# A two-layer transformer kernel on one NeuronCore: the last tile of each layer norm in two token halves

## The reference, cut to what matters

```
mod = silu(c) @ w_ada[l] + b_ada[l]            # six vectors of 1024: sh1, sc1, g1, sh2, sc2, g2
h = x * (1 + sc1) + sh1
y = token_mixer(h, ...)                        # ends in merged @ w_out
x = layer_norm(ALPHA * x + g1 * y, ln1_g, ln1_b)
h = x * (1 + sc2) + sh2
y = conv_ffn(h, ...)                           # ends in u @ w_down, 2816 rows
x = layer_norm(ALPHA * x + g2 * y, ln2_g, ln2_b)

def layer_norm(x, g, b):                       # over the 1024 features of each token
    mu = mean(x); var = mean((x - mu) ** 2)
    return (x - mu) * rsqrt(var + 1e-5) * g + b
```

## Time and profile before

| | |
|---|---|
| median of 3 runs | 2410.18 us (2404.59 to 2410.34) |
| profiled execution | 2407.2 us, its span 2404.8 us |
| TensorE busy | 2337.0 us, 97% of the span |
| VectorE, ScalarE, GpSimd busy | 1265.6 (53%), 992.3 (41%), 995.6 (41%) us |
| mean granted TensorE clock | 0.997 |
| DMA | 259.54 MB, mean 108 GB/s |

### The profile page before, as it was taken

One profiled execution on the slowest core, in us unless ns is written; L12 is line 12 of the kernel. 1 busy time (PEld: TensorE's weight loads), 2 busy tenths in 40 slices (PEclk: granted clock), 3 DMA queues, 4 the chain that ended last, 5 costly groups with the idle time before them and its releaser, 6 DMA issues.

```text
span 2404.8 us, 32261 instructions
## 1 busy us (share of the span) xinstructions
PE 2337.0 (97%) x11392; PEld 1866.7 (78%) x11392; DVE 1265.6 (53%) x2662; ACT 992.3 (41%) x1649; POOL 995.6 (41%) x808
## 2 busy tenths in 40 slices
PE   6999999999999999999999999999999999999988
PEld 4778778878888876887787888887888867778756
DVE  7575675654445356657567434314640163276684
ACT  6444445344343244544534343423142344333463
POOL 3343222454444443423244544444544434454342
PEclk9999999999999999999999999999999999999999
DMA  8532134322226334212442232223232221222210
GB/s 332 214 123 71 61 115 158 123 73 102 93 88 236 106 149 160 97 36 88 144 146 96 88 105 89 88 96 112 88 105 87 102 78 36 87 88 88 88 45 36
DMA packets 51843, 259.54 MB, mean 108 GB/s; under 512 B 6352, under 2 KB 16080, under 8 KB 26128
## 3 DMA queue, kind: packets, MB, share of 16 engines
q1 hardware_dynamic: 50576, 249.63, 29.9%
q0 software_dynamic: 1152, 8.39, 0.8%
HBM read 249.47 MB, written 7.34 MB: 107 GB/s over the span
## 4 chain that ended last, share of the span: by engine, by line
PE 77%; issue 11%; POOL 5%; DVE 4%; ACT 2%; DMA 1%; SPq 0%; POOLq 0%; DVEq 0%; ACTq 0%
PE bank L738 22%; PE bank L740 21%; PE bank L739 21%; POOL w_lo L595 4%; PE bank L986 2%; PE bank L899 1%; PE bank L1225 1%; PE bank L991 1%; PE bank L1028 1%; PE bank L888 1%; PE bank L874 1%; PE bank L929 1%; PE bank L1214 1%; PE bank L1377 1%; DMA ada_early<-w_ada 0%
## 5 line engine op out<-in xcount | busy, mean ns | idle before, releaser
L595 POOL TENSOR_TENSOR w_lo<-w_raw,w_hi 128x512 fp32r<-128x512 f32 (+1 forms) x684 | 873.1, 1308 | 1208.3 <-ACT w_hi L1429 815.6
L738 PE MATMUL bank<-h_hi,w_hi 128*128 128x512 f32 x1616 | 647.0, 400 | 11.5 <-ACT gates_b L1509 5.6
L740 PE MATMUL bank<-h_hi,w_lo 128*128 128x512 f32 x1616 | 631.4, 391 | 0.0
L739 PE MATMUL bank<-h_lo,w_hi 128*128 128x512 f32 x1616 | 629.8, 390 | 0.0
L738 PEld LDWEIGHTS bank<-h_hi,w_hi 128*128 128x128 f32 x1616 | 304.3, 188 | 85.4 <-issue 18.4
L740 PEld LDWEIGHTS bank<-h_hi,w_lo 128*128 128x128 f32 x1616 | 303.7, 188 | 64.9
L739 PEld LDWEIGHTS bank<-h_lo,w_hi 128*128 128x128 f32 x1616 | 304.4, 188 | 58.3 <-issue 0.5
L1429 ACT ACTIVATE w_hi<-w_raw 128x2048 fp32r<-128x2048 f32 (+2 forms) x112 | 197.6, 1764 | 280.5 <-PE bank L740 227.6
L2293 DVE SCALAR_TENSOR_TENSOR cv<-bank,par,cv 128x511 f32<-128x511 f32 (+1 forms) x176 | 131.6, 749 | 213.4 <-ACT cv L1685 200.4
L1434 ACT ACTIVATE w_hi<-w_raw 128x2048 fp32r<-128x2048 f32 x68 | 129.9, 1910 | 125.5 <-PE bank L740 117.0
L1685 ACT ACTIVATE cv<-bank,par 128x512 f32<-128x512 f32 x88 | 68.3, 779 | 233.4 <-PE bank L740 232.1
(11 more groups left out here) (385 smaller groups left out, 3841.1 us busy)
## 6 DMA issues: line engine op xcount, KB each, us to landing
w_raw<-w_stream SPq DMA_DIRECT2D x150, 1024.0 KB, 4.9
w_raw<-w_down SPq DMA_DIRECT2D x32, 704.0 KB, 4.0
ada_mid<-w_ada SPq DMA_DIRECT2D x20, 1024.0 KB, 5.4
ada_last<-w_ada SPq DMA_DIRECT2D x12, 1024.0 KB, 4.9
ada_early<-w_ada POOLq DMA_DIRECT2D x8, 1024.0 KB, 20.8
ada_late<-w_ada SPq DMA_DIRECT2D x8, 1024.0 KB, 6.3
bias_in<-bias_scratch SPq DMA_DIRECT2D x16, 256.0 KB, 3.0
bias_in<-bias_scratch SPq DMA_DIRECT2D x16, 192.0 KB, 2.7
```

The source lines that it names most:

```text
L595: ins = nc.gpsimd.tensor_tensor(w_lo[r][:, part], w_raw[r][:, part], w_hi[r][:, part].bitcast(fp32), ALU.subtract)
L738: nc.tensor.matmul(out, w[0][:, cols], xh, start=first, stop=False)
L739: nc.tensor.matmul(out, w[0][:, cols], xl, start=False, stop=False)
L740: return nc.tensor.matmul(out, w[1][:, cols], xh, start=False, stop=last)
```

## The change

Tile 7 is computed in two halves of 256 tokens, each to its end, in different banks. For each half DVE adds the residual, then adds it to `ln_shift`; ACT squares the half; DVE adds the square to `ln_mean`. `norm_early` is gone: behind the tile one set of sums is made from the complete `ln_shift` and `ln_mean`, by token for the first half and then for the second, then 512 columns for the mean. In the second norm, DVE adds the first slot's part of tile 7 as a whole while the second slot runs in halves.

In the tail, ACT copies the next slot's high part in four pieces of 512 columns, one behind each of the first four high parts of the activation, and POOL subtracts the mean from tiles 2 to 7 rather than 3 to 7.

In the first norm of a layer, the group behind tile 5 makes four sums; the other eight (gate columns 40 to 47) are made in the tail where the last five warming products were, and DVE takes them after the tail. `ada_take` and `affine` move ahead of the residual of tile 6.

```diff
 # GpSimd, norm_sub
-                for f in range(3, KD):
+                for f in range(2, KD):
...
 # TensorE
-            def tile(out, w, at, xh, xl, ks, k0=0, first=True, last=True):
+            def tile(out, w, at, xh, xl, ks, k0=0, first=True, last=True, tok=slice(0, S)):
                 for k in range(ks):
-                    ins = mm3(out, w, slice(at + k * P, at + (k + 1) * P), xh[:, k0 + k, :], xl[:, k0 + k, :],
+                    ins = mm3(out, w, slice(at + k * P, at + (k + 1) * P), xh[:, k0 + k, tok], xl[:, k0 + k, tok],
                               first and k == 0, last and k == ks - 1)
...
-            def norm_early(l, which):
-                k = 2 * l + which
-                pe.wait_ge(zcsum_ready, k + 1)
-                nc.tensor.matmul(banks[5][:, :], mean_w, ln_shift[:, :], start=True, stop=False)
-                by_token(4, ln_shift)
-                pe.wait_ge(sq_used, KD * k + 7)
-                by_token(3, ln_mean).then_inc(early_done, 1)
...
                 elif f == 7:
-                    pe.wait_ge(tile_evac, tdone(l, t + 6))
-                    keep_warm(0, 3)
-                    pe.wait_ge(tile_evac, tdone(l, t + 7))
-                    by_token(2, x[:, 7, :]).then_inc(tok_done, 1)
-                    pe.wait_ge(sq_ready, KD * (k + 1))
-                    by_token(7, ln_sq[1]).then_inc(sq_used, 1)
-                    nc.tensor.matmul(banks[5][:, :], mean_w, x[:, 7, :], start=False, stop=True).then_inc(rest_done, 1)
+                    for c in range(2):
+                        pe.wait_ge(zcsum_ready, 4 * k + 2 + 2 * c)
+                        ins = by_token(2, ln_shift, HALF_BLOCKS[c])
+                        if c:
+                            ins.then_inc(tok_done, 1)
+                            pe.wait_ge(sq_used, KD * (k + 1))
+                        else:
+                            pe.wait_ge(zcsum_ready, 4 * k + 3)
+                        ins = by_token(7, ln_mean, HALF_BLOCKS[c])
+                    ins.then_inc(tok_done, 1)
+                    nc.tensor.matmul(banks[5][:, :], mean_w, ln_shift[:, :], start=True, stop=True).then_inc(rest_done, 1)
                     pe.wait_ge(inv_ready, k + 1)
...
-                    keep_warm(0, 5)
+                    if which:
+                        keep_warm(0, 5)
+                    else:
+                        pe.wait_ge(ada_used, 2 * (12 * l + 12))
+                        ada_products(6, 2, 0, 7).then_inc(ada_sum, 1)
...
                     else:
-                        tile(banks[1][:, :], split(l, SLOT_OUT + 3), D, m_hi, m_lo, 5, last=False)
-                        norm_early(l, 0)
-                        ins = tile(banks[1][:, :], split(l, SLOT_OUT + 3), D + 5 * P, m_hi, m_lo, 3, 5, first=False)
+                        for c in range(2):
+                            if c:
+                                pe.wait_ge(tile_evac, tdone(l, TILE_OUT + 6))
+                            ins = tile(banks[1 - c][:, HALF[c]], split(l, SLOT_OUT + 3), D, m_hi, m_lo, KD, tok=HALF[c])
+                            if c == 0:
+                                ins.then_inc(half_done, 1)
...
-                        ada_group(12 * l + 9, 3, 0, 6)
+                        ada_group(12 * l + 9, 1, 0, 6)
...
+                        if f == 7 and s:
+                            for c in range(2):
+                                if c:
+                                    pe.wait_ge(part_added, 3 * l + 2)
+                                else:
+                                    pe.wait_ge(tile_evac, tdone(l, TILE_DOWN + 6))
+                                tile(banks[c][:, HALF[c]], split(l, SLOT_DOWN + s), 0, u_hi, u_lo, 11, 11, tok=HALF[c]
+                                     ).then_inc(tile_done if c else half_done, 1)
...
 # ScalarE, norm_tail
-                split_hi(l, *split_after)
                 act.wait_ge(gb_ready, k + 1)
+                n = slot_no(l, split_after)
+                act.wait_ge(w_full[n % 2], 16 * (n // 2 + 1))
                 for j in range(KD):
                     act.wait_ge(zn_ready, k * KD + j + 1)
                     A_(h_hi[:, j, :], banks[2 + j % 2][:, :], ACT.Identity, bias=ln_gb[:, 8 + j:9 + j]).then_inc(h_hid, 1)
+                    if j < 4:
+                        part = slice(512 * j, 512 * j + 512)
+                        ins = A_(w_hi[n % 2][:, part], w_raw[n % 2][:, part], ACT.Copy)
+                        if j == 3:
+                            ins.then_inc(w_hi_done, 1)
...
 # VectorE, in place of the residual of tile 7
+            def last_residual(l, which, t):
+                k = 2 * l + which
+                scale = mod[l][:, 23 + 24 * which:24 + 24 * which]
+                if which:
+                    dve.wait_ge(half_done, HALVES * (l + 1) - 1)
+                    V.scalar_tensor_tensor(x[:, 7, :], banks[1][:, :], scale, x[:, 7, :], ALU.mult, ALU.add
+                                           ).then_inc(part_added, 1)
+                    dve.wait_ge(part_added, 3 * l + 2)
+                dve.wait_ge(zcsum_ready, 4 * k + 1)
+                dve.wait_ge(sq_used, KD * k + 7)
+                for c in range(2):
+                    at = HALF[c]
+                    if c:
+                        dve.wait_ge(tile_done, tdone(l, t + 7))
+                    else:
+                        dve.wait_ge(half_done, HALVES * l + (2, HALVES)[which])
+                    V.scalar_tensor_tensor(x[:, 7, at], banks[c if which else 1 - c][:, at], scale, x[:, 7, at], ALU.mult,
+                                           ALU.add).then_inc(tile_evac if c else part_added, 1)
...
+                    V.tensor_tensor(ln_shift[:, at], x[:, 7, at], ln_shift[:, at], ALU.add).then_inc(zcsum_ready, 1)
+                    dve.wait_ge(sq_ready if c else sq_half, KD * (k + 1) if c else k + 1)
+                    V.tensor_tensor(ln_mean[:, at], ln_sq[1][:, at], ln_mean[:, at], ALU.add
+                                    ).then_inc(sq_used if c else zcsum_ready, 1)
...
 # VectorE, norm_tail
-                        if f >= 3:
-                            dve.wait_ge(zs_ready, 5 * k + f - 2)
+                        if f >= 2:
+                            dve.wait_ge(zs_ready, 6 * k + f - 1)
...
-                    if f == 7:
+                    if f == 6:
                         ada_take(l, 2)
                         affine(l, 0)
...
                 norm_tail(l, 0)
+                dve.wait_ge(ada_sum, 4 * l + 4)
+                chain(V.tensor_tensor(mod[l][:, 40:48], banks[7][:, 0:256:32], par[l][:, 40:48], ALU.add))
```

More of the change, by code:

```diff
@@ L49 @@
  TILE_DOWN, TILES) = (0, 8, 16, 24, 28, 32, 40, 44, 52, 60, 68, 76, 120, 128)
-HALVES = 9
+HALVES = 11
 SLOT2_Q, SLOT2_V, SLOT2_GATE, SLOT2_OUTA, SLOT2_K2, SLOT2_V2, SLOT2_Q2, SLOT2_G2, SLOT2_OUTB, SLOTS2 = (
@@ L339, in build @@
         var_ready = sem("var_ready")
-        early_done = sem("early_done")
+        part_added = sem("part_added")
+        sq_half = sem("sq_half")
         tok_done = sem("tok_done")
@@ L441, in build @@
                ("k", 3)]
+        HALF, HALF_BLOCKS = (slice(0, S // 2), slice(S // 2, S)), (range(2), range(2, NB))
         OUT_FIRST = (7, 4)
@@ L774, in keep_warm, with ada_products @@
                     nc.tensor.matmul(banks[bank][:, 0:P], ones, ident, start=True, stop=True)
-            def ada_group(first, halves, late, bank):
-                pe.wait_ge(ada_used, 2 * (first + halves))
-                part = first % 12 - 4 if first % 12 else 0
+            def ada_products(part, halves, late, bank):
                 for j in range(4 * halves):
@@ L782, in ada_group @@
                                            ones[:, 0:32], start=True, stop=True)
-                ins.then_inc(ada_sum, 1)
+                return ins
+            def ada_group(first, halves, late, bank):
+                pe.wait_ge(ada_used, 2 * (first + halves))
+                ada_products(first % 12 - 4 if first % 12 else 0, halves, late, bank).then_inc(ada_sum, 1)
             pe.sem_inc(tile_done, TILE_PRE)
@@ L925, in stat, with by_token @@
                 return nc.tensor.matmul(banks[bank][:, :], w, src, start=(f == first), stop=(f == KD - 1))
-            def by_token(bank, src):
-                for b in range(NB):
+            def by_token(bank, src, blocks):
+                for b in blocks:
                     ins = nc.tensor.matmul(banks[bank][:, b * P:(b + 1) * P], src[:, b * P:(b + 1) * P], mean_w,
@@ L1145, in down @@
                             wait_bank(l, TILE_DOWN + f, 2)
[L1146 to L1149, removed]
+                        if f == 7 and s:
[7 more added lines that the diff above has]
+                        else:
+                            ins = tile(banks[f % 2][:, :], split(l, SLOT_DOWN + s), 0, u_hi, u_lo, 11, 11 * s, s == 0,
+                                       s == 1 or f == 7)
+                            ins.then_inc(tile_done if s else half_done, 1)
                 for f in range(KD):
```

(35 more changed lines are left out.)

18 lines of the change are left out of this document (8 added, 10 removed).

## The result

The changed kernel takes 2389.02 us (median of four runs, 2388.77 to 2390.99) against 2409.82 for the kernel before (2404.59 to 2410.34): ratio 0.992, 95% interval 0.9903 to 0.9938. Timed once more later: 2388.34 against 2405.8, ratio 0.9926 (0.9913 to 0.994), which is 17.5 us. The profiled execution took 2389.18 us (span 2387.0) where the one of before took 2407.2. The forecast was 2392.

What follows compares the result with a forecast made beforehand. Most of the kernel was taken to be a TensorE stream, 77% of the span. First norms 4.45 and second norms 3.83, twice each, take 16.6 us off 2407.2, so 2390.6; forecast 2392, range 2385 to 2397.

Steps and rivals of the forecast that it cites:

- steps 1 and 2: Last tile of each norm: no early sums, gain 2.56 us; two halves, cost 0.31 us (first norms) or 0.43 (second).
- step 3: First norm of each layer: 16 of 24 narrow products behind tile 5 move into the gap, gain 0.5 us.
- the margin at the second half: First norm's last tile: DVE done with the first half at 474.9, TensorE with the second at 475.5, margin 0.6 us.
- steps 4 and 5: Each norm: shorter tail to the variance, gain 0.7 us; weight split in pieces and POOL's extra subtraction, gain 1.0 us.
- Halves do not fall back: Last tile: 256-column products not half the time of whole ones; 2409 at 0.20 us (chance 0.07), 2455 at 0.40 (0.04).
- DVE is held by POOL: Last tile: POOL holds DVE's first-half sums 1.1 us each, giving 2398; chance 0.13 together with nothing from steps 4 and 5.
- The clock did not fall behind a gap: Rival, gap behind the last tile: granted clock falls to 0.50, 1.4 us each at two norms, so 2395; chance 0.08.
- the basis: Time of the kernel before: profiled 2407.2, 3.0 below the median 2410.18; 2390.6 from the profiled one, forecast 2392.

Runs made afterwards that it cites:

- gates_early: The changed kernel with all 24 narrow products behind tile 5 of each first norm again, ten warming products in the gap: 2390.02 us.
- whole_tile: The changed kernel with the last tile of each norm whole again, one set of sums behind it: 2393.68 us.
- best: The changed kernel with 32 narrow products split, tile 4's residual ahead of DVE's centring, gate sum and affine coefficients in DVE's waits behind the last residual: 2383.92 us.
- pool_later: The changed kernel with POOL's low part in second norms held until DVE's two first-half sums are done: 2392.15 us.
- widths: The changed kernel with 96 more fp32r products of eight widths in one gap of layer 0's first norm: spacing 0.228 us at 512 columns, 0.120 at 256.
- copy_whole: The changed kernel with ACT copying the 2048-column weight whole ahead of the high parts: next slot 0.45 us later in norms 1, 2 and 4.

## Why the prediction was right

**Early sums, split (steps 1 and 2): right.** The end of the last tile came 2.76 us sooner behind the narrow products, forecast 2.56 - 0.31 + 0.5 = 2.75. That the two agree to 0.01 is partly luck: the late gate columns gave 0.40 of it and not 0.5, and the early sums cost TensorE 2.36 + 0.32 = 2.68 (gates_early and whole_tile) and not the 2.56 of the pause itself. No run puts the early sums back into the change; the 2.68 is a difference of timelines. The split cost 0.32 us (whole_tile), forecast 0.31, and 0.43 in norm 4, forecast 0.43; the form that no row showed takes 0.120 us, as assumed. The Trainium skill ("TensorE: Matmul & The Clock Gate", "Back-to-back issue gap") would make the split cost 48 x 0.098 - 24 x 0.131 = 1.56 us, an estimate from its figures; the measurement disagrees and decides.

**Late gate columns (step 3): right in kind, a little too large.** 0.39 us instead of 0.5 per first norm; the rest is the 1.23 us wait for DVE that the forecast named, and best shows that it can be had. What the step got wrong is a margin: the gate columns and affine coefficients do not fit ahead of the residual of tile 6. From 469.58 on they take DVE 1.46 us, forecast about 1; the tile's last product ends at 470.37 + 0.39 = 470.76, and DVE starts the residual at 471.04 with no wait, so about 0.25 us late. With another 0.20 between DVE's last sum of squares and the first half's residual, for which the forecast had nothing, the margin at the second half is 0.20 us instead of 0.6. It cost nothing, but little was left.

**Tail and pieces (steps 4 and 5): right.** 2.27 us from residual to variance, forecast 2.3. From the tile's end to the next slot it takes 18.28 us instead of 20.02: 1.74 less, forecast 1.7. The parts add up to 1.67: 0.70 from the tail, 0.45 from the pieces and 0.52 from POOL's sixth subtraction. POOL's low part ends at 493.55, 1.24 us ahead of the next slot, forecast 1.2.

**The rivals.** Halves do not fall back. DVE is held by POOL in the second norms as feared, by 1.07 us a sum, and still has 0.41 us to spare. The forecast had judged the hold against the first norm's margin of 0.6; in norm 2 DVE waits 2.41 us for the second half when the first half's sums are not held (pool_later), which also shows the price where the hold is not covered. The two sums from which the forecast inferred the hold differ in their operands as well, the short one reading a bank; pool_later compares like with like. The clock did not fall behind a gap in any norm of the change's two profiles; it did once in four norms where 0.9 us were added to the gap, and once in two where its warming products went. The Trainium skill (same page, "HAM oscillation") says that long enough idle gaps of TensorE are followed by matmuls at half clock; the traces agree in part, since like gaps went either way. The falls at the 32 narrow products had no idle time of TensorE ahead of them; why they come in some executions and not in others stays open.

**The total.** 16.6 us were forecast and 17.0 measured: 4.50 and 4.52 in the first norms (forecast 4.45), 3.96 and 4.00 in the second (forecast 3.83). The rest of the distance from 2392 to 2389 is the basis: three runs of before had a median of 2410.18, and I leaned to it from the profiled 2407.2; later medians were 2405.8 to 2407.18. The 20.8 us of the first comparison hold some of that scatter, and the profiles' 18.0 a fall of 1.6 that only one of them had.

## What to carry to other kernels

Price a split by the spacing of the narrower products and by what the half saves in the serial tail: 0.3 us of stream bought 1.4 us of tail. Removing work ahead of a wait is worth only what the next waiter lets through; look there for the next edit, here the residual that DVE did too late. Before explaining a gain by an edit, profile the same kernel twice: a fall of the clock of 1.6 us sat in one of two executions.

## What the runs showed of the hardware

- In widths, fp32r products follow each other at 0.228 us with 512 columns and 0.120 with 256; the 256 columns between cost 0.108 us, about a column per cycle of the 2.4 GHz level. From 224 columns down to 64 they need 0.111 to 0.112 whatever the width. So a last tile in quarters of 128 columns would take about 96 x 0.111 = 10.7 us of TensorE instead of 48 x 0.120 = 5.8, an estimate from these rows.
- A DVE sum of two SBUF operands of 256 columns takes 0.42 to 0.43 us while POOL stands still and 1.19 to 1.51 while POOL subtracts. The Trainium skill ("SBUF — State Buffer", "SBUF: two separate sides") says that DVE and GpSimd share a port pair which one instruction holds to its end; these traces agree, POOL's instruction being 5.06 / 4 = 1.27 us long.
- The clock fell to 0.50 at 32 narrow products of 32 columns in a row in eight of eleven profiles, with TensorE busy ahead of it and throughout. Behind 24 or fewer of them it fell once, in copy_whole, where 1.01 us of idle time lay between.
